# The root of the norm leaves the input of four feed-forward stages and multiplies their gate and up tiles

## The reference, cut to what matters

```python
def rmsnorm(x, g):
    y = xf * lax.rsqrt(jnp.mean(xf * xf, axis=-1, keepdims=True) + EPS)
    return y * g

def swiglu_ffn(h, w_up, w_down):
    a, b = jnp.split(h @ w_up, 2, axis=-1)
    return (jax.nn.silu(a) * b) @ w_down

for l in range(2):                                            # first block
    x = x + 0.5 * swiglu_ffn(rmsnorm(x, ffn1_norm[l]), ffn1_w_up[l], ffn1_w_down[l])
    x = x + mixer(rmsnorm(x, mix_norm[l]), ...)
    x = x + 0.5 * swiglu_ffn(rmsnorm(x, ffn2_norm[l]), ffn2_w_up[l], ffn2_w_down[l])
    x = rmsnorm(x, final_norm[l])
```

## Time and profile before

| | |
|---|---|
| time, median of 3 runs | 2469.99 us (2464.59 to 2470.62) |
| the profiled execution's own time | 2465.53 us |
| its span, first to last instruction | 2463.7 us |
| mean granted TensorE clock | 0.962 of full speed |
| busy: PE, DVE, ACT | 94%, 70%, 48% |

### The profile page before, as it was taken

How to read it: one execution, slowest core, us unless ns; L and a number is a source line. 1 busy time by engine, 2 the same in 40 slices (tenths; PEclk the granted TensorE clock), 3 DMA queues, 4 the chain that set the end, 5 groups by cost and what they waited for, 6 DMA issues and landing times.

```text
span 2463.7 us, 45856 instructions
## 1 busy us (share of the span) xinstructions
PE 2325.4 (94%) x18250; PEld 2254.4 (92%) x18250; DVE 1728.3 (70%) x2811; ACT 1192.4 (48%) x1752; POOL 51.0 (2%) x100
## 2 busy tenths in 40 slices
PE   7999999999998999999998999899898899798997
PEld 6999999988998999999998999798887899797997
DVE  6666889857667766888966766686445777666676
ACT  5444444555444444443454544436444565444563
POOL 0000000000000000000000000000000000000000
PEclk9999999999999999999999999898789999998999
DMA  7776434235775777543424677343112455353552
GB/s 286 238 237 207 163 121 143 85 118 183 241 238 188 247 236 237 177 142 117 140 78 145 214 239 239 118 160 101 68 61 77 131 185 179 112 174 110 186 179 94
DMA packets 110431, 406.03 MB, mean 165 GB/s; under 512 B 12256, under 2 KB 12384, under 8 KB 109920
## 3 DMA queue, kind: packets, MB, share of 16 engines
q1 hardware_dynamic: 96192, 352.33, 42.3%
q0 software_dynamic: 13824, 50.34, 6.7%
q10 hardware_dynamic: 288, 1.57, 0.2%
HBM read 403.14 MB, written 1.05 MB: 164 GB/s over the span
## 4 chain that ended last, share of the span: by engine, by line
PE 88%; DVE 8%; ACT 3%; issue 1%; DMA 0%; DVEq 0%; ACTq 0%; SPq 0%
PE bank L488 87%; DVE w_lo L1356 1%; PE bank L628 1%; DVE arena L1519 1%; ACT w_hi L970 1%; DVE rinv L1390 1%; DVE work L1425 1%; DVE work L1393 0%; ACT rinv L991 0%; ACT work L1109 0%; DVE rinv L1422 0%; ACT arena L1248 0%; DVE h_lo L1384 0%; ACT work L989 0%; DMA tabs<-shape_tables 0%
## 5 line engine op out<-in xcount | busy, mean ns | idle before, releaser
L488 PE MATMUL bank<-h_hi,w_hi 128*128 128x256 f32 x3968 | 1163.0, 294 | 60.1 <-ACT h_hi L997 27.9
L488 PE MATMUL bank<-h_hi,w_lo 128*128 128x256 f32 x3968 | 1140.5, 288 | 0.0
L488 PE MATMUL bank<-h_lo,w_hi 128*128 128x256 f32 x3968 | 1106.8, 285 | 0.0
L1356 DVE TENSOR_TENSOR w_lo<-w_raw,w_hi 128x1024 fp32r<-128x1024 f32 x663 | 808.9, 1223 | 378.3 <-ACT w_hi L970 371.9
L970 ACT ACTIVATE w_hi<-w_raw 128x1024 fp32r<-128x1024 f32 x663 | 699.6, 1057 | 662.3 <-PE bank L488 656.7
L488 PEld LDWEIGHTS bank<-h_hi,w_hi 128*128 128x128 f32 x3968 | 781.3, 197 | 82.8 <-issue 58.8
L488 PEld LDWEIGHTS bank<-h_hi,w_lo 128*128 128x128 f32 x3968 | 781.3, 197 | 0.0
L488 PEld LDWEIGHTS bank<-h_lo,w_hi 128*128 128x128 f32 x3968 | 758.6, 194 | 5.1 <-issue 5.0
L488 PE MATMUL bank<-hid_hi,w_hi 128*128 128x256 f32 (+1 forms) x1104 | 314.6, 285 | 9.4 <-ACT arena L1174 2.9
L488 PE MATMUL bank<-hid_lo,w_hi 128*128 128x256 f32 (+1 forms) x1104 | 312.7, 283 | 0.0
L488 PE MATMUL bank<-hid_hi,w_lo 128*128 128x256 f32 (+1 forms) x1104 | 312.5, 283 | 0.0
(11 more groups left out here) (216 smaller groups left out, 1899.4 us busy)
## 6 DMA issues: line engine op xcount, KB each, us to landing
w_raw<-weights SPq DMA_DIRECT2D x663, 512.0 KB, 3.3
mod_w_buf<-mod_w POOLq DMA_DIRECT2D x96, 512.0 KB, 4.7
tabs<-shape_tables SPq DMA_DIRECT2D x1, 1746.0 KB, 14.4
work<-v_bias ACTq DMA_DIRECT2D x2, 768.0 KB, 4.7
x<-x_fm SPq DMA_DIRECT2D x1, 1024.0 KB, 4.7
out_fm<-x SPq DMA_DIRECT2D x1, 1024.0 KB, 3.9
vecs<-vectors SPq DMA_DIRECT2D x1, 712.0 KB, 7.3
tabs<-shape_tables SPq DMA_DIRECT2D x1, 65.0 KB, 4.6
```

The source lines that it names most:

```text
L488: ins = pe.matmul(o, lhs, rhs, start=start, stop=stop, skip_group_check=share)
L1356: v.tensor_tensor(w_lo[:, n % SPLIT, :], w_raw[:, n % RAW, :], w_hi[:, n % SPLIT, :].bitcast(F32), ALU.subtract).then_inc(lo_ready[n % SPL ...
```

## The change

In the four feed-forward stages of the first block the input is x times the gain of the norm, without the root. ACT writes `h_hi` straight from x with the gain as its scale (`norm_later`), and DVE writes `h_lo` from x (`low_later`). The squares are taken after that, and the mean square is made on PE between pair 0 and pair 1 of the stage. ACT splits weight tiles up to tile 4 before it waits for the mean square. DVE splits them too before it inverts the root. In every step DVE multiplies the gate half and the up half of the bank by `rinv` (`scaled_hidden`), ACT takes Silu of the product in place, and the rest is as before. The first two steps of ACT's loop are written out ahead of the loop, in the second block's stages as well. At the first entry the first two weight tiles are split ahead of the norm.

```diff
@@ PE, ffn() @@
                 column_pair(h_ready, None)
+                if mod:
+                    mean_squares()
                 column_pair(None, None)
                 down(0, 0)
@@ PE, first block @@
             for l in range(DEPTH):
-                mean_squares()
                 ffn(True)
                 mean_squares()
                 mod_cols()
                 first_mixer(l)
-                mean_squares()
                 ffn(True)
@@ ACT @@
+            def norm_later(ready, gain):
+                if ready is res_pair:
+                    act.wait_ge(ready, w.next(ready, KT // 2))
+                for kt in range(KT):
+                    if kt % 2 == 0 and ready is x_ready:
+                        act.wait_ge(ready, w.next(ready))
+                    act_f(h_hi[:, kt, :], x[:, kt, :], ACT.Identity, scale=gain[:, kt:kt + 1]).then_inc(h_high, 1)
+                w.skip(h_ready, KT)
+                for kt in range(KT):
+                    act_f(work[:, kt, :], x[:, kt, :], ACT.Square).then_inc(sq_ready, 1)
+                high_parts(state["tile"] + 4)
+                act.wait_ge(stat_full, w.next(stat_full))
+                act_f(rinv[:, :], half(6, 0), ACT.Sqrt, bias=tab("eps")).then_inc(root_ready, 1)
...
             def plain_step(par, t):
-                act.wait_ge(pair_full, w.next(pair_full))
-                act_f(gate_a[:, par, :], half(UP + par, 0), ACT.Silu).then_inc(gate_ready, 1)
+                act.wait_ge(gate_scaled, w.next(gate_scaled))
+                act_f(gate_a[:, par, :], gate_a[:, par, :], ACT.Silu).then_inc(gate_ready, 1)
...
             for l in range(DEPTH):
-                norm(None if l == 0 else x_ready, None)
                 if l == 0:
                     act.wait_ge(vecs_loaded, w.next(vecs_loaded, 16))
-                    high_parts(2)
+                    high_parts(1)
+                norm_later(None if l == 0 else x_ready, vec("ffn1_norm", l, 0, KT))
+                if l == 0:
                     first_vectors()
-                ffn_steps(plain_step)
+                ffn_steps(plain_step, (gate_scaled,), 4)
                 first_mixer(l)
-                norm(res_pair, None)
-                ffn_steps(plain_step)
+                norm_later(res_pair, vec("ffn2_norm", l, 0, KT))
+                ffn_steps(plain_step, (gate_scaled,), 4)
@@ DVE @@
+            def low_later(gain):
+                for kt in range(KT):
+                    dve.wait_ge(h_high, w.next(h_high))
+                    v.scalar_tensor_tensor(h_lo[:, kt, :], x[:, kt, :], gain[:, kt:kt + 1], h_hi[:, kt, :].bitcast(F32),
+                                           ALU.mult, ALU.subtract).then_inc(h_ready, 1)
...
+            def scaled_hidden(par):
+
+                g, u, b = gate_a[:, par, :], fpad[:, par, SHORT_TAPS - 1:], UP + par
+                dve.wait_ge(pair_full, w.next(pair_full))
+                v.tensor_tensor(g, half(b, 0), rinv[:, :], ALU.mult).then_inc(gate_scaled, 1)
+                v.tensor_tensor(u, half(b, 1), rinv[:, :], ALU.mult).then_inc(dve_link, 1)
+                dve.wait_ge(dve_link, w.next(dve_link))
+                dve.wait_ge(gate_ready, w.next(gate_ready))
+                v.tensor_tensor(hid_hi[:, par, :], g, u, ALU.mult)
+                v.tensor_tensor(g, g, u, ALU.mult).then_inc(dve_link, 1)
...
                 else:
+                    low_parts(t0 + 4)
+                    dve.wait_ge(root_ready, w.next(root_ready))
+                    v.reciprocal(rinv[:, :], rinv[:, :]).then_inc(dve_link, 1)
+                    dve.wait_ge(dve_link, w.next(dve_link))
                     for j in range(FT):
-                        hidden(j % 2)
+                        scaled_hidden(j % 2)
...
             for l in range(DEPTH):
-                norm(vec("ffn1_norm", l, 0, KT))
+                if l == 0:
+                    low_parts(1)
+                low_later(vec("ffn1_norm", l, 0, KT))
                 if l == 0:
                     low_parts(2)
                     first_vectors()
```

More of the change, by code:

```diff
@@ L355, in build @@
         y_down = sem("ffn_output_bank_taken")
+        gate_scaled = sem("gate_tile_scaled")
         gate_ready = sem("activated_gate_ready")
@@ L1005, in split_high, with ffn_steps @@
                     act_f(h_hi[:, i:i + 2, :], raw[:, i:i + 2, :], ACT.Copy).then_inc(high_ready, 1)
-            def ffn_steps(step):
+            def ffn_steps(step, turned, tiles):
                 t0 = state["tile"]
[L1011 to L1014, removed]
+                high_parts(t0 + tiles)
+                for j in range(2):
+                    step(j, t0 + 3 * j)
+                    high_parts(t0 + 3 * j + 5)
+                with act.Fori(0, FT // 2 - 2) as i:
+                    w.turn(i, [(s, 2) for s in turned] + [(w_used, 6)] + [(s, 16) for s in w_full])
                     for j in range(2):
[L1016 to L1019, removed]
+                        step(j, t0 + 3 * j + 6)
+                        high_parts(t0 + 3 * j + 11)
+                w.turned(FT // 2 - 2)
+                state["split"] += 3 * (FT - 6)
                 for j in range(FT - 2, FT):
@@ L1022, in ffn_steps @@
                     high_parts(min(t0 + 3 * j + 5, t0 + 3 * FT + 1))
+                if pair_full not in turned:
+                    w.skip(pair_full, FT)
                 state["tile"], state["pair"] = t0 + 3 * FT, state["pair"] + FT
             def plain_step(par, t):
-                act.wait_ge(pair_full, w.next(pair_full))
-                act_f(gate_a[:, par, :], half(UP + par, 0), ACT.Silu).then_inc(gate_ready, 1)
+                act.wait_ge(gate_scaled, w.next(gate_scaled))
+                act_f(gate_a[:, par, :], gate_a[:, par, :], ACT.Silu).then_inc(gate_ready, 1)
             def conv_step(par, t):
@@ L1310, in _ @@
                 norm(x_ready, modv[:, l, 3, :])
-                ffn_steps(conv_step)
+                ffn_steps(conv_step, (pair_full, gate_convolved), 2)
                 squares(y, y_down)
@@ L1442, in hidden @@
                                 ).then_inc(hid_ready, 1)
+            def scaled_hidden(par):
[8 more added lines that the diff above has]
+                dve.wait_ge(dve_link, w.next(dve_link))
+                v.tensor_tensor(hid_lo[:, par, :], g, hid_hi[:, par, :].bitcast(F32), ALU.subtract
+                                ).then_inc(hid_ready, 1)
             def gate_conv(par, j, at_w, at_b):
@@ L1491, in ffn_steps @@
                 state["tile"] = t0 + 3 * FT
-                w.skip(pair_full, FT)
+                if at:
+                    w.skip(pair_full, FT)
                 state["pair"] += FT
@@ L1954, in _ @@
                 first_mixer(l)
-                norm(vec("ffn2_norm", l, 0, KT))
+                low_later(vec("ffn2_norm", l, 0, KT))
                 ffn_steps()
```

## The result

| | before | after |
|---|---|---|
| time, median (lowest to highest) of 12 runs each | 2467.57 us (2464.59 to 2470.99) | 2473.48 us (2468.09 to 2477.82) |
| the profiled execution's time, its span | 2465.53, 2463.7 us | 2473.29, 2471.5 us |
| mean granted TensorE clock | 0.962 | 0.961 |

What follows compares the result with a forecast made beforehand. PE, busy 94% of the span, was taken as the bound. Entry terms 2.7 + 4.8 + 2.9 - 5.2 gave 5.2 us less, so 2467.7 - 5.2 = 2462.5 us, range 2456 to 2470.

Steps and rivals of the forecast that it cites:

- The first entry: Layer 0's ffn1: PE starts 6.3 us earlier, then waits 5.3 for low part 3; stage 5.2 us late by down 1.
- Rival (b): First entry costs little, or other ramps are priced too dear: gain of 10.4 us, 2457 us; chance 0.27.
- So 0.2 us is given back: First steps of the three later stages: DVE, short of time, delivers low part 7 at 606.8, wanted at 606.6.
- rival (c): Clock falls in three later entries, up to 1.7 us each: gain between 3.5 and nothing, 2464 to 2468 us; chance 0.12.
- The rest of an entry: Later entries: 16.5 us from addition to down 0 in ffn2; ffn1 of layer 1 gains 5.0 us before 0.2 is returned.
- 88 steps cost nothing: First block's feed-forward steps: DVE's added work stays hidden while less than 2.4 us is added, steps 8.59 us apart.
- rival (d): Steps begin to wait on the chain from pair to low part: 0.15 us in 88 steps, 13 us, 2475 us; chance 0.07.

Runs made afterwards that it cites:

- e2: Changed kernel, with the small Silu and Exp ahead of the root on ACT at the first entry: 2465.56 us, ratio 0.9987 to the kernel before.
- e9: Changed kernel, second mod tiles moved to steps 3 and 12, one unread DVE operation of that size added in steps 0 and 1: 2467.28 us.
- e3: Changed kernel, Exp ahead of the root at the first entry, second mod tiles of steps 0 and 1 at steps 3 and 12: 2455.24 us.
- e7: e3 with no mod tile at a stage's last step, taken at step 9 instead: 2454.18 us, ratio 0.9946 to the kernel before.
- e10: e9 with a second extra unread DVE operation in step 1: 2468.87 us, ratio 1.0002 to the kernel before.
- e4: Kernel before with its old norm, only the two new multiplications added in each step, by a column of ones: 2473.11 us, ratio 1.0023.
- e6: Kernel before, only mod tiles moved: second ones to steps 3, 9 and 12, none at the last step: 2469.36 us, ratio 1.0003.
- e8: e7 plus filler matmuls that nobody reads, in pair 0 and ahead of it in ffn2 stages: 2458.92 us, ratio 0.9968 to the kernel before.

## Why the prediction was wrong, by its own steps

- **The first entry** (down 0 at 40.8, PE waiting 5.3 us for the low part of tile 3): right but for 0.8 us. The wait was 5.23 us at 36.33, down 0 at 41.62. The hidden tile was ready at 41.31, and PE was the later one: it took tile 3 at the low clock from 36.33 to 41.62, which the prediction had down as nothing beside the wait. e2 shows the cause that was named: with the Exp ahead of the root the whole loss goes. Rival (b) is out. The Trainium skill, "ScalarE: Activation LUTs", section "Table sets: the hidden batching unit", prices a switch at about 2.7 us, and the trace does not agree: the load took 1.28 us, and from the end of the small Silu (30.27) to the start of the Exp (31.58) passed 1.31. The 1283 ns that the prediction sets beside it, from the Trainium skill's "What ACT_TABLE_LOAD costs" on the same page, are the load alone; that section adds a drain of about 1380 ns, and with it the two figures are one. Its rule to keep functions of a set together is not what e2 tested: e2 has as many loads up to the first step's Silu (five) and gains by their place.
- **"So 0.2 us is given back"**: this step failed, in three stages. DVE's own chain was worked out well. From the end of hidden tile 0 to the low part of tile 7 it gave 9.9 us; in e9, with the same work and no DMA to wait for, it took 9.76, and a stage lost 0.24 us (0.9 the first). In the changed kernel it took 10.8, 11.8, 10.8 and 10.0. What it left out is the refill of the buffer behind it: I took the mod tiles from a stage where they came in time (2.60), and didn't ask when the fourth could land, nor what its being late would cost once DVE had no slack. It was allowed 0.2 us in each of three stages and measured 3.8, 1.3 and 0.5; the first stage's steps had been given 1.2 and took 2.0. This is 5.8 of the 12.5 us.
- **The clock in the entries** was rival (c), at 0.12. Its mechanism came true, in 13 of 14 ffn2 entries. It was priced at up to 1.7 us; two ffn2 entries cost 1.0 each, and ffn1 of layer 1 had 6.8 us of low clock where e2, e3, e7 and e10 had 3.4 and took 0.6 to 1.3 us less. Against it I had set one row, a wait of 2.0 us behind which the clock stayed up. In e4 and e6, with the same instructions at that place, it did fall behind it. The rule of the Trainium skill, "TensorE: Matmul & The Clock Gate", section "HAM oscillation", that waits between bursts of matmuls put the clock down again and again, was borne out, here behind waits of 1.42 us in 13 cases of 14; one row was too little against it. The rival's own price does not reach the result: at most 2468 us, for 2473.48.
- **The rest of an entry** was right. In e3, layer 0, where the clock held, the addition's end to down 0 was 16.8 us for 16.5 forecast; its ffn1 of layer 1, with the 3.4 us of low clock of before, gained 4.5 of 5.0 (19.2 to 14.7 us from the end of the final norm).
- **The ends of the stages** were not in the sum. The prediction put them at nothing without a reason. Behind the last hidden tile DVE has a low part, a mod tile and another low part ahead of the additions to x: 0.34 us each, 1.4 in all. Timeline of DVE in the changed kernel:

```profile
221.33 1.22 DVE L1376 TENSOR_TENSOR w_lo<-w_raw,w_hi 128x1024 fp32r<-128x1024 f32 x1
222.46 1.28 DVE L1734 SCALAR_TENSOR_TENSOR mod_w_buf<-mod_w_buf,c_act 128x1024 f32<-128x1024 f32 x1
223.66 1.22 DVE L1376 TENSOR_TENSOR w_lo<-w_raw,w_hi 128x1024 fp32r<-128x1024 f32 x1
224.80 1.88 DVE L1542 SCALAR_TENSOR_TENSOR x<-bank,x 128x512 f32<-128x512 f32 x3
```

  The four run without a gap, so DVE is the bound; with the mod tile gone (e7) the end is that of before.
- **"88 steps cost nothing"**: right for the steps between (8.59 us, rival (d) did not come), wrong as a sum, since the first steps and the last have no cover.

Not settled: what sets off a fall of the clock beyond the wait before it, in the entries and in mixers whose instructions are alike, and why one mod tile lands after 4.6 us and another after 7.2.

## What to carry to other kernels

Where work is added to a loop whose steady part has slack, count it in the first and last steps, where the queue is full, and ask of every buffered input there when its refill can be issued, not only when the engine is free. The change pays once two things around it move: e7, the Exp ahead of the root and the second mod tiles at steps 3, 9 and 12, with none at the last step, has the lowest median (2454.18 us, 0.54% less than before), though it can't be told from e3 (0.51%). Anything that needs a table of its own and feeds an in-order queue belongs ahead of a wait on PE, not behind it.

## What was unexpected of the hardware

- A mod tile of 512 KB landed after 3.7 to 3.9 us when issued to idle DMA engines, and the next, issued 1.3 us later, after 4.9 to 7.0. In the kernel before, with 5 us for the first of the two (4.6 to 5.6), the second took 4.6 to 7.2.
- The same wait of PE (1.42 us for the first high part, then two matmuls behind each) left the clock up in e3 at 582.53 and put it down 13 other times, with the same instructions around it. In one and the same kernel the falls at the entries repeated in each of three profiles.
- With the same second block, low clock in it ran from 133 us (the changed kernel and e10) to 150 us (e8), and its length from 897.4 (e10) to 902.9 us (e8). A gain of a few us in one place can be lost there by where the rest of the program comes to lie.
